# Expert gate and up products with the weights stationary and 96 slots moving, and four more weight tiles

## The reference, cut to what matters

```python
def _hier_moe(h, p):
    ...
    g_logit = (x @ p["router_group_w"] + p["router_group_b"]).astype(F32)
    ...
    e_top, e_sel = lax.top_k(e_in, TOP_K_EXPERT)            # 2 of the 4 experts of the token's group
    w = jax.nn.softmax(e_top, axis=-1) * p_group
    ...
    hg = jnp.einsum('nd,edf->nef', x, p["w_gate"])          # [1024] -> [256], per expert
    hu = jnp.einsum('nd,edf->nef', x, p["w_up"])
    a = jax.nn.silu(hg) * hu * combine.astype(x.dtype)[..., None]
    y = jnp.einsum('nef,efd->nd', a, p["w_down"])           # [256] -> [1024]
```

## Time and profile before

| | us |
|---|---|
| median of 3 runs | 1421.64 |
| lowest and highest | 1420.54, 1421.66 |
| profiled execution | 1426.84 |
| its span | 1425.0 |
| first expert's gate and up to the last down, layer 0 | 521.94 to 707.71 |
| the same, layer 1 | 1196.89 to 1382.67 |

### The profile page before, as it was taken

One profiled execution on the slowest core, in us unless ns is written; L12 is line 12 of the kernel. 1 busy time (PEld: TensorE's weight loads), 2 busy tenths in 40 slices (PEclk: granted clock), 3 DMA queues, 4 the chain that ended last, 5 costly groups with the idle time before them and its releaser, 6 DMA issues.

```text
span 1425.0 us, 16091 instructions
## 1 busy us (share of the span) xinstructions
PE 1201.4 (84%) x6399; PEld 938.5 (66%) x6399; DVE 525.3 (37%) x1159; ACT 360.4 (25%) x753; POOL 141.7 (10%) x194
## 2 busy tenths in 40 slices
PE   2499989999998669999808998999999857999970
PEld 0277768898856457777506776888985645777750
DVE  1234453434354442222144335434435443222214
ACT  2232235432202301111123222454230230111101
POOL 5000020000000021111034001000000001111102
PEclk9999999999999879999958999999999987999995
DMA  9956651136822248999948666012542224999954
GB/s 282 247 180 233 194 196 60 60 119 208 268 89 89 89 162 321 363 370 359 339 138 189 212 202 195 31 60 64 176 150 89 97 91 155 330 364 373 370 211 147
DMA packets 133052, 280.45 MB, mean 197 GB/s; under 512 B 7024, under 2 KB 89104, under 8 KB 120688
## 3 DMA queue, kind: packets, MB, share of 16 engines
q1 hardware_dynamic: 114896, 219.12, 44.9%
q0 software_dynamic: 17472, 58.66, 12.5%
q10 hardware_dynamic: 608, 1.62, 0.3%
HBM read 253.68 MB, written 25.69 MB: 196 GB/s over the span
## 4 chain that ended last, share of the span: by engine, by line
PE 79%; DMA 8%; DVE 7%; ACT 3%; issue 2%; POOL 0%; SPq 0%; DVEq 0%; POOLq 0%; ACTq 0%
PE ps L996 16%; PE ps L789 14%; PE ps L660 14%; PE ps L1015 8%; PE ps L913 6%; PE ps L926 5%; DMA ring<-in_ada_w 3%; PE ps L773 3%; PE ps L573 2%; DMA ring<-in_w_in 2%; PE ps L984 2%; PE ps L736 2%; DMA scratch_ys<-arena 1%; PE ps L679 1%; PE ps L621 1%
## 5 line engine op out<-in xcount | busy, mean ns | idle before, releaser
L996 PE MATMUL ps<-ring,arena 128*128 128x256 f32 x1024 | 226.5, 379 | 4.0 <-ACT arena L1944 4.0
L996 PEld LDWEIGHTS ps<-ring,arena 128*128 128x128 f32 x1024 | 194.2, 190 | 43.0 <-issue 13.4
L471 DVE TENSOR_TENSOR w_lo<-ring,w_hi 128x512 fp32r<-128x512 f32 x128 | 88.2, 692 | 174.6 <-ACT w_hi L460 174.6
L460 ACT ACTIVATE w_hi<-ring 128x512 fp32r<-128x512 f32 x128 | 80.3, 631 | 284.0 <-PE ps L660 152.4
L789 PE MATMUL ps<-h_hi,w_hi 128*128 128x384 f32 x384 | 135.4, 353 | 5.7 <-DVE w_lo L468 3.0
L468 DVE TENSOR_TENSOR w_lo<-ring,w_hi 128x512 fp32r<-128x512 f32 x96 | 67.2, 702 | 194.3 <-ACT w_hi L458 194.3
L789 PE MATMUL ps<-h_hi,w_lo 128*128 128x384 f32 x384 | 129.8, 338 | 0.0
L789 PE MATMUL ps<-h_lo,w_hi 128*128 128x384 f32 x384 | 129.7, 338 | 0.0
L660 PE MATMUL ps<-w_hi,h_hi 128*128 128x512 f32 x288 | 117.0, 406 | 9.2 <-DVE w_lo L471 5.9
L1015 PE MATMUL ps<-ring,arena 128*128 128x512 f32 x256 | 115.6, 594 | 2.8 <-DVE arena L1675 2.8
L660 PE MATMUL ps<-w_lo,h_hi 128*128 128x512 f32 x288 | 113.9, 395 | 0.0
(11 more groups left out here) (268 smaller groups left out, 1641.7 us busy)
## 6 DMA issues: line engine op xcount, KB each, us to landing
ring<-in_ada_w SPq DMA_DIRECT2D x48, 1024.0 KB, 7.9
ring<-in_w_in SPq DMA_DIRECT2D x48, 1024.0 KB, 5.4
ring<-in_w_gate SPq DMA_DIRECT2D x32, 1024.0 KB, 7.2
ring<-in_w_up SPq DMA_DIRECT2D x32, 1024.0 KB, 8.7
ring<-in_w_down SPq DMA_DIRECT2D x32, 1024.0 KB, 8.0
scratch_ys<-arena POOLq DMA_DIRECT2D x32, 512.0 KB, 7.9
ring<-in_w_out SPq DMA_DIRECT2D x8, 1024.0 KB, 5.1
gb<-in_ada_b POOLq DMA_DIRECT2D x8, 512.0 KB, 5.0
```

What stands on the lines that cost most here:

```text
L460: eng.activation(w_hi[:, q % 2], ring[:, slot, 2 * q:2 * q + 2, :], ACT.Copy).then_inc(whi_ready, 1)
L471: eng.tensor_tensor(w_lo[:, q % 2], ring[:, SLOT[seg, l, c], 2 * q:2 * q + 2, :], w_hi[:, q % 2].bitcast(F32), ALU.subtract).then_inc(wlo_ ...
L996: mm = pe.matmul(ps[:, 2 + e % 2, w * CH:(w + 1) * CH], hgT[:, e % 2, k, :], ring[:, SLOT[name, l, e], k, :], start=(k == 0), stop=(k == K ...
```

## The change

The slots of a block go from 128 to `CAP` = 96, and the further blocks from 5 to 7. In gate and up the weights become stationary, in two halves of 128 columns, and the 96 slots move. The result is [hidden, slot] at once, so `activations_turned`, its copy, `act_a` and `aTs` go. Down is kept, with 96 stationary columns; it alternates between two pairs of PSUM banks. The hidden dimension of `w_down` is laid out as (j p) in place of (p j), so that it fits the order of the halves. Four more weight tiles serve the experts: two in `arena`, two in `biasT`. Expert tiles go round over eight places, others over the four of the ring as before. The small routing tiles move to another place in `arena`.

```diff
+CAP = 96
+EXTRA = 7
+ALL_BLOCKS = N_EXP + EXTRA
...
+EXPERT_SLOTS = SLOTS + 4
+def slots():
+    slot, turn, expert = {}, 0, 0
+    for item in ORDER:
+        if item[0] in ("gate", "up", "down"):
+            at = expert % EXPERT_SLOTS
+            slot[item] = SLOTS + at if at < EXPERT_SLOTS - SLOTS else (turn + at - (EXPERT_SLOTS - SLOTS)) % SLOTS
+            expert += 1
+        else:
+            slot[item] = turn % SLOTS
+            turn += 1
+    return slot
...
+        def slot_tile(slot):
+            if slot < SLOTS:
+                return ring[:, slot]
+            n = slot - SLOTS
+            at = arena[:, 10496 + 2048 * n:10496 + 2048 * (n + 1)] if n < 2 else biasT[:, 2048 * (n - 2):2048 * (n - 1)]
+            return at.rearrange("p (k c) -> p k c", k=KT)
...
-                    return a["w_down"][l, item[2]].rearrange("(p j) c -> p j c", j=2)
+                    return a["w_down"][l, item[2]].rearrange("(j p) c -> p j c", j=2)
...
             def put(item):
-                if SEQ[item] >= SLOTS:
-                    sp.wait_ge(chunk_done, SEQ[item] - SLOTS + 1)
+                if EARLIER[item]:
+                    sp.wait_ge(chunk_done, SEQ[EARLIER[item]] + 1)
                 slot = SLOT[item]
+                if item == ("gate", item[1], 0):
+                    sp.wait_ge(chunk_done, SEQ["br", item[1], 3] + 1)
+                    sp.wait_ge(br_read, item[1] * 8 + 8)
...
-                        mm = pe.matmul(ps[:, 0, 128:150], at_lane[:, k, t, :], at_block[:, k, t, :],
+                        mm = pe.matmul(ps[0:CAP, 0, 128:128 + ALL_BLOCKS], at_lane[:, k, t, :], at_block[:, k, t, :],
...
+                def expert_hidden(bank, part, par, w):
+                    for j in range(2):
+                        for k in range(KT):
+                            mm = pe.matmul(ps[:, bank, (2 * part + j) * CAP:(2 * part + j + 1) * CAP], w[:, k, j * P:(j + 1) * P],
+                                           hgT[:, par, k, :], start=(k == 0), stop=(k == KT - 1))
+                    return mm
+                def expert_output(bank, half, par, w):
+                    wd = w.rearrange("p k c -> p (k c)").rearrange("p (j n) -> p j n", n=D)
+                    for j in range(2):
+                        mm = pe.matmul(ps[0:CAP, bank, :], aT[:, par, j * CAP:(j + 1) * CAP], wd[:, j, half * 512:(half + 1) * 512],
+                                       start=(j == 0), stop=(j == 1))
+                    return mm
...
                 def gate_up(e):
-                    if e:
+                    if e >= 2:
                         pe.wait_ge(a_made, blocks(l, e))
-                    for w, name in enumerate(("gate", "up")):
+                    for part, name in enumerate(("gate", "up")):
                         loaded((name, l, e))
-                        for k in range(KT):
-                            mm = pe.matmul(ps[:, 2 + e % 2, w * CH:(w + 1) * CH], hgT[:, e % 2, k, :], ring[:, SLOT[name, l, e], k, :],
-                                           start=(k == 0), stop=(k == KT - 1))
-                        mm.then_inc(chunk_done, 1)
-
-                def activations_turned(e):
+                        expert_hidden(2 + e % 2, part, e % 2, slot_tile(SLOT[name, l, e])).then_inc(chunk_done, 1)
+
+                def down(e):
                     pe.wait_ge(a_made, blocks(l, e) + 2)
-                    for j in range(2):
-                        mm = pe.transpose(ps[:, 4, j * P:(j + 1) * P], act_a[:, e % 2, j:CH:2], ident)
-                    mm.then_inc(aT_psum, 1)
-
-                def down(e):
-
-                    pe.wait_ge(aTs_ready, blocks(l, e) + 1)
-                    pe.wait_ge(y_act, blocks(l, e) + 1)
-                    pe.wait_ge(y_dve, blocks(l, e) + 1)
+                    if e >= 2:
+                        pe.wait_ge(y_act, blocks(l, e))
+                        pe.wait_ge(y_dve, blocks(l, e))
                     loaded(("down", l, e))
...
-                link(dve.scalar_tensor_tensor(out=e16[:, 0, :], in0=counts, scalar=2 * P + 0.5, in1=e16[:, 0, :],
-                                              op0=ALU.is_gt, op1=ALU.add))
+                for n in (2, 3):
+                    linked()
+                    link(dve.scalar_tensor_tensor(out=e16[:, 0, :], in0=counts, scalar=n * CAP + 0.5, in1=e16[:, 0, :],
+                                                  op0=ALU.is_gt, op1=ALU.add))
...
                 def inputs_copied(e):
                     dve.wait_ge(xgT_psum, blocks(l, e) + 1)
-                    dve.tensor_copy(hgT[:, e % 2, 4:8, :].rearrange("p k n -> p (k n)"), ps[:, 1, :]).then_inc(hg_dve, 1)
+                    if e >= 2:
+                        done(("up", l, e - 2))
+                    dve.tensor_copy(hgT[:, e % 2, 4:8, :].rearrange("p k n -> p (k n)"), ps[:, 1, 0:4 * CAP]).then_inc(hg_dve, 1)
...
-                    done(("up", l, e))
-                    dve.tensor_tensor(act_a[:, par], act_t[:, par], ps[:, 2 + par, CH:2 * CH], ALU.mult).then_inc(a_made, 1)
+                    if e >= 2:
+                        done(("down", l, e - 2))
+                    dve.tensor_tensor(aT[:, par], act_t[:, par], ps[:, 2 + par, 2 * CAP:4 * CAP], ALU.mult).then_inc(a_made, 1)
-                def activations_copied(e):
-                    dve.wait_ge(aT_psum, blocks(l, e) + 1)
-                    dve.tensor_copy(aTs[:, e % 2].rearrange("p j n -> p (j n)"), ps[:, 4, 0:CH]).then_inc(aTs_ready, 1)
...
-                    pool.dma_start(a["ys"][b * P:(b + 1) * P], yb[:, b % 4, :]).then_inc(y_stored, 16)
+                    pool.dma_start(a["ys"][b * CAP:(b + 1) * CAP], yb[:, b % 4, :]).then_inc(y_stored, 16)
```

More of the change, by code:

```diff
@@ L81 @@
 SEQ = {item: n for n, item in enumerate(ORDER)}
-SLOT = {item: n % SLOTS for item, n in SEQ.items()}
+EXPERT_SLOTS = SLOTS + 4
[10 more added lines that the diff above has]
+    return slot
+SLOT = slots()
 LOADED = {}
-_loads = [0] * SLOTS
+EARLIER = {}
+_loads = [0] * EXPERT_SLOTS
+_last = [None] * EXPERT_SLOTS
 for _item in ORDER:
@@ L87 @@
     LOADED[_item] = _loads[SLOT[_item]]
+    EARLIER[_item] = _last[SLOT[_item]]
+    _last[SLOT[_item]] = _item
 BIAS_W = P + 6 * GRID_W
@@ L105 @@
 C_BLOCKS = 1386
-C_END = 1408
-C_MASKF, C_MASKB, C_DIFFF, C_DIFFB = 1408, 1536, 1664, 1792
-C_ALL = 1920
+C_END = 1412
+C_MASKF, C_MASKB, C_DIFFF, C_DIFFB = 1412, 1540, 1668, 1796
+C_ALL = 1924
 def constants():
@@ L207, in build @@
[L207 to L212, removed]
+        xg = arena[0:CAP, 0:4096].rearrange("p (b c) -> p b c", b=4)
+        yb = arena[0:CAP, 4096:8192].rearrange("p (b c) -> p b c", b=4)
@@ new lines, in build @@
+        hgT = arena[:, 8192:8192+16*CAP].rearrange("p (b k n) -> p b k n", b=2, k=KT)
+        act_t = arena[:, 9728:9728+4*CAP].rearrange("p (b c) -> p b c", b=2)
+        aT = arena[:, 10112:10112+4*CAP].rearrange("p (b c) -> p b c", b=2)
+        hotsum = arena[:, 4096:4144].rearrange("p (t e) -> p t e", e=16)
+        e16 = arena[:, 4144:4208].rearrange("p (n e) -> p n e", e=16)
+        owner = arena[:, 4208:4208 + 16 * EXTRA].rearrange("p (n e) -> p n e", e=16)
+        ownerf = arena[:, 4320:4320 + EXTRA]
@@ new lines, in build @@
+        r16 = arena[:, 4328:4520].rearrange("p (n t e) -> p n t e", n=4, t=TILES)
+        lo = arena[:, 4520:4580].rearrange("p (t c) -> p t c", t=TILES)
+        rmod = arena[:, 4608:4656].rearrange("p (t e) -> p t e", e=16)
+        hot_rmod = arena[:, 4656:4752].rearrange("p (k t e) -> p k t e", k=2, e=16)
+        lane = arena[:, 4752:4758].rearrange("p (k t) -> p k t", k=2)
+        first = arena[:, 4758:4764].rearrange("p (k t) -> p k t", k=2)
+        at_lane = arena[:, 4768:4768 + 6 * CAP].rearrange("p (k t n) -> p k t n", k=2, t=TILES)
@@ L295, in build @@
         act_init = sem("act_init")
-        slot_loaded = [sem(f"slot_loaded{i}") for i in range(SLOTS)]
+        slot_loaded = [sem(f"slot_loaded{i}") for i in range(EXPERT_SLOTS)]
         chunk_done = sem("chunk_done")
@@ L974, in _, with expert_inputs @@
                 broadcast_moe_gate(l)
+                def expert_inputs(src):
+                    for k in range(KT):
+                        mm = pe.transpose(ps[:, k // 4, (k % 4) * CAP:(k % 4 + 1) * CAP], src[:, k * P:(k + 1) * P],
+                                          cst[0:CAP, C_IDENT:C_IDENT + CAP])
+                    return mm
+                def expert_hidden(bank, part, par, w):
+                    for j in range(2):
+                        for k in range(KT):
+                            mm = pe.matmul(ps[:, bank, (2 * part + j) * CAP:(2 * part + j + 1) * CAP], w[:, k, j * P:(j + 1) * P],
[6 more added lines that the diff above has]
+                                       start=(j == 0), stop=(j == 1))
+                    return mm
                 def inputs_turned(e):
@@ L1611, in _ @@
                 linked()
-                link(dve.scalar_tensor_tensor(out=r16[:, 1], in0=rank, scalar=P - 0.5, in1=bcast(e16[:, 3, :], [P, TILES, 16], 1),
```

(12 more changed lines are left out.)

134 lines of the change are left out of this document (49 added, 85 removed).

## The result

The changed kernel takes 1409.32 us (median of 4 runs, 1407.97 to 1412.35); the kernel before takes 1421.09 us beside it (4 runs, 1419.7 to 1421.66). The ratio is 0.9922, with a 95% interval of 0.9904 to 0.994. It is faster, by 11.8 us. The forecast was 5.6 us and its range ended at 1411, so the direction was right and the gain is twice as large.

The account below looks back on a forecast made before the run. TensorE was taken as the bound, busy 160.38 of 160.40 us over layer 0's experts. Terms of -3.2 us in layer 0 and -2.4 in layer 1 gave -5.6 us, so 1416.0 us from a median of 1421.64, range 1411 to 1420.5.

Parts of the forecast that it names:

- Input transposes stay at 0.87 us: Eight input transposes per expert: no saving, because their weight load still has 128 columns.
- the ends of the layers: Last gate record to first gather: about 3.5 us saved in layer 0, 2.7 in layer 1.
- Gate and up: Per expert: 64 load-bound records at 0.1117 us, 7.15 us against 6.90 before.
- The swap a wash and the tiles worth nothing: Per expert: gates and removed turned activations net +0.02 us; four more weight tiles bring nothing, as TensorE never waits.
- Routing: Before the experts: two more comparisons +0.45 us, narrower stationary tile -0.66 us, sum -0.2 us per layer.
- Second expert: TensorE's wait for VectorE's chain before the second expert: 0.25 us shorter per layer.
- The fifteenth down and the last: Layer end: fifteenth down directly after the gates, -0.67 us per layer; last 3.44 us later, -1.15 us in layer 1 only.
- The stores: Result stores at layer end, taken to go mostly by bytes: -2.4 us in layer 0, -0.4 us in layer 1.
- No change: Rival, chance 0.13: layer 0's stores do not shorten and loads run at 0.1125 us, giving 1420.0 us.
- Columns setting the pace: Rival, chance 0.05: gate and up products at 81 ns, experts then bound by DMA, giving 1382 us.
- The clock: Rival, chance 0.05: granted clock halves in the expert stage, making it slower, 1637 us if all loads fell.
- The extra pass: Rival, chance 0.04: an expert exceeds 96 tokens and seven passes run, +140 us in a layer, 1556 us.

Follow-up runs that it names:

- e1: The changed kernel with input transposes taking 128 rows and 128 identity columns again, 32 stale rows unused: 1415.84 us, ratio 0.9959 to the kernel before.
- e4: The kernel before with 96 slots in place of 128, no operand swap, four tiles: 1411.77 us, ratio 0.9931 to the kernel before.
- e3: The changed kernel with 128 slots and five further blocks, operand swap and eight tiles kept: 1421.85 us, ratio 1.0008 to the kernel before.
- e2: The changed kernel without the four further weight tiles for the experts: 1409.82 us, ratio 0.9913 to the kernel before.
- e5: The changed kernel with POOL waiting for each store one block later, so the last two stores overlap: 1409.38 us, ratio 0.9913 to the kernel before.
- e7: The changed kernel with each block stored from 128 partitions, 32 stale rows included and overwritten by the next block: 1411.87 us (one run).
- e6: The changed kernel with 64 of 96 slots in input transposes and gate and up, output not the reference's: 1441.98 us (one run).
- e8: The changed kernel with SyncE asking for the next layer's first weight tiles only after layer 0's result gathers: 1409.05 us, ratio 0.9907 to the kernel before.
- e9: The changed kernel with the edits of e5 and e8 together: 1403.12 us, ratio 0.9879 to the kernel before.

## Why the prediction was right in direction and wrong in size

**The step that failed** is "Input transposes stay at 0.87 us, since their weight load still has 128 columns". I had found that the load sets the pace of float32 products and carried it over to transposes, though the earlier trace rows show them at 0.87 / 8 = 0.109 us with 128 moving columns, which suits either reading: load and column pace meet at that size. The moving columns went from 128 to 96 with the slots, and the distance from 0.109 to 0.082 us. Fifteen sets of 0.21 us in each layer are 6.3 us, as much as the whole miss; e1 gives it back alone (6.0 us), and e4 has it without the swap. The other terms were off too, and it is luck that they nearly cancel: routing gave 0.7 us more than forecast and the gates 1.0 more, the ends of the layers 2.0 less and the second expert 0.3 less.

"TensorE: Matmul & The Clock Gate" of the Trainium skill, section "LDWEIGHTS (loading the stationary operand)", gives a load as its columns over 1.2, an estimate of 107 ns for 128, and names no exception. The traces speak against it on both sides: 111 to 112 ns from load to load in the stream of products, and transposes 82 and 62 ns apart whose load has the same 128 columns.

**Gate and up: right.** 7.12 us against 7.15 forecast and 6.90 before. Load-bound, shown at 64, 96 and 128 moving columns. The 0.03 us too many are 0.5 us per layer.

**The swap a wash and the tiles worth nothing: right.** e3 gives 1.0008, and e2 the changed kernel's time. The forecast took the earlier trace rows for sixteen experts; the stretch holds fourteen periods, which changes nothing in the reading. DMA is at 0.91, under the 0.93 named.

**Routing: direction right, size small.** Line 1001 falls by 0.64 us (0.66 forecast). VectorE's chain ahead of it is 0.35 us longer, where I had 0.45 for the added comparisons. The whole stage is 0.65 and 0.47 us shorter where I had 0.2, but its length varies: e5, which has the same routing, takes 42.1 us in layer 0 where the changed kernel takes 40.74. So the 0.2 to 0.4 us beyond the two terms are not shown to come from the change.

**Second expert:** about 0.1 us in place of 0.25.

**The fifteenth down and the last: right in place.** They start at 688.97 and 692.41, the first straight behind the gates, the last 3.44 us later.

**The stores: over-estimated, and not shown to go by bytes.** In layer 0 they fall from 12.91 to 11.28 us, 1.6 where I took 2.4. But with 512 KB e3 has 10.56 us there and e7 12.21, and with 384 KB e4 has 9.71 and e1 12.70. The sum varies by 3 us between kernels of one size, so the 1.6 us can't be put down to the smaller stores. They land in 5.42 and 5.86 us, where I had named 4.5 to 5.5. In layer 1 I named the last down and then one store of 2.5 us as what is late next. In fact the fifteenth's store is: it takes 3.23 us, not less than 2.93, and the last store can't be issued before it has landed. So the 1.15 us of the last down are worth little, and the tail gives 1.43 us where I had 2.7. By bytes a lone store would have shrunk; by its measured time it did not (e7).

**The rivals.** No change is out. Columns setting the pace was wrong for products (e6) and right for the transposes: the one place where I did not ask it. The clock stayed full in the changed kernel's profiled execution and fell at 64 columns. It was not safe at 96 either: in e5 (layer 0) and e8 (layer 1) it cost 1.6 us. The extra pass did not run: the gate line has 2048 records, what sixteen experts in two layers need.

**What stays open:** whether the transposes' pace goes by the moving columns or by the rows of the stationary tile, which shrank with them in every run (the record of its load stays at some 0.14 us with 128, 96 and 64 rows); what makes the stores of layer 0 vary; how much of e9's gain over e8 is more than differences between executions; and whether e3's longer routing stage belongs to that kernel or to its profiled execution.

## What to carry to other kernels

Work out the pace of each kind of instruction from rows of its own kind: in one stage the weight load set the pace of the products, and the number of slots that of the transposes. When a change narrows a tile, list every instruction that touches it, also those whose line reads as unchanged in the argument, and ask for each which side bounds it. Where one of two serial transfers leaves the chain's end, look at the transfer before it and at what shares its engines; waiting to ask for the next stage's tiles, with the two stores overlapped, was worth another 6 us by the medians, 5.3 of them seen in the stretch they touch.

## What the runs showed of the hardware

- Loads of a 128-column float32 stationary tile come every 0.111 to 0.112 us in a stream of products with 64, 96 or 128 moving columns (e6, the changed kernel, e3); in a stream of transposes of 64 slots they come every 0.062 us (e6). The weight load's record is itself shorter there:

```profile
L1012 PEld LDWEIGHTS ps<-cst,arena x256: 137/140/173, 514.1 to 1346.2; 96*128 96x128 f32 x128
```

  This view counts each line's loads with ns minimum, median and maximum. The median is 140 ns, where the page has a mean of 192 for line 1020.
- With 64 moving columns behind 128-column loads the granted clock was 0.54 over 27.4 us and 0.50 over 29.4 us at the start of the two layers' experts (e6); with 96 it was 1.00 in the changed kernel, and 0.76 over some 7 us once each in e5 and e8.
- Twelve products with 96 stationary columns took 2.08 us at half clock, with 128 columns 2.72 (changed kernel, e3).
- A lone store of 384 KB from 96 partitions took 3.23 us, one of 512 KB from 128 partitions 2.90 (changed kernel, e7).
- Two stores of 384 KB took 5.42 and 5.86 us while weight tiles of 1024 KB were landing, and 3.22 and 4.19 us when these were asked for later (changed kernel, e8).
